# Moving the next expert's token gather one chunk earlier, and its one-hot transposes behind it, in a mixture-of-experts decoder kernel

## The reference

```
def moe_ffn(h, router_w, wg, wu, wd):
    B, S, D = h.shape
    t = h.reshape(B * S, D)
    logits = (t @ router_w).astype(jnp.float32)
    top_vals, top_idx = lax.top_k(logits, TOP_K)
    gates = jax.nn.softmax(top_vals, axis=-1)
    combine = jnp.sum(jax.nn.one_hot(top_idx, N_EXPERTS, dtype=jnp.float32) * gates[..., None], axis=1)
    y = jnp.zeros((B * S, D), jnp.float32)
    for e in range(N_EXPERTS):
        y = y + combine[:, e:e + 1] * swiglu(t, wg[e], wu[e], wd[e]).astype(jnp.float32)
    return y.astype(h.dtype).reshape(B, S, D)
```

## Time and profile before

| | |
|---|---|
| median of 3 runs | 1327.45 us (1326.04 to 1327.48) |
| span of the profiled execution | 1324.5 us |
| profiled execution's own time beside its span | not listed apart; the median of the runs is 2.95 us above the span |
| PE busy with matmuls | 1248.4 us, 94% |
| DVE busy | 1011.2 us, 76% |
| ACT busy | 793.3 us, 60% |
| first gate matmul of expert 0 | at 493.29 us |

### The profile page before, as it was taken

The page is one execution under the profiler, slowest core; times in us unless marked ns, Lnnn a source line. Parts: engine busy times, 40 slices in busy tenths (PEclk is TensorE's granted clock), DMA queues, the critical chain, the costliest instruction groups (busy, mean ns, idle before and its releaser), DMA issues.

```text
span 1324.5 us, 16360 instructions
## 1 busy us (share of the span) xinstructions
PE 1248.4 (94%) x6062; PEld 1037.6 (78%) x6062; DVE 1011.2 (76%) x988; ACT 793.3 (60%) x710; POOL 0.2 (0%) x4
## 2 busy tenths in 40 slices
PE   6998999999999869999999999989999998999996
PEld 4787788889787758887887887877887886887885
DVE  6878664444685778789788788887889886888885
ACT  4455354434446347677677677666667665667663
POOL 0000000000000000000000000000000000000000
PEclk9999899999999889999999999999999998999998
DMA  9842245546563138899899899898989998989970
GB/s 359 306 159 96 95 161 188 159 128 199 169 225 115 59 100 308 274 354 376 278 335 399 280 343 386 286 336 309 313 299 379 330 306 313 333 285 380 349 259 35
DMA packets 158798, 343.19 MB, mean 259 GB/s; under 512 B 5824, under 2 KB 47040, under 8 KB 158720
## 3 DMA queue, kind: packets, MB, share of 16 engines
q1 hardware_dynamic: 158720, 342.10, 74.3%
HBM read 341.02 MB, written 1.05 MB: 258 GB/s over the span
## 4 chain that ended last, share of the span: by engine, by line
PE 83%; DVE 10%; ACT 4%; issue 2%; DMA 0%; SPq 0%; DVEq 0%; ACTq 0%
PE ps L415 26%; PE ps L417 25%; PE ps L416 25%; DVE wlo L290 5%; ACT whi L283 3%; PE ps L644 1%; PE ps L465 1%; DVE scaled L1114 1%; PE ps L766 1%; PE ps L767 1%; PE ps L440 1%; PE ps L741 1%; PE ps L740 1%; DVE stlo L1124 1%; PE ps L514 0%
## 5 line engine op out<-in xcount | busy, mean ns | idle before, releaser
L290 DVE TENSOR_TENSOR wlo<-raw,whi 128x2048 fp32r<-128x2048 f32 (+3 forms) x356 | 741.3, 2100 | 237.6 <-ACT whi L283 237.2
L283 ACT ACTIVATE whi<-raw 128x2048 fp32r<-128x2048 f32 (+3 forms) x356 | 625.5, 1765 | 342.8 <-PE ps L417 341.3
L415 PE MATMUL ps<-whi,sthi 128*128 128x512 f32 (+4 forms) x1232 | 468.9, 381 | 21.7 <-DVE wlo L290 14.4
L417 PE MATMUL ps<-whi,stlo 128*128 128x512 f32 (+4 forms) x1232 | 457.9, 372 | 3.6 <-issue 3.6
L416 PE MATMUL ps<-wlo,sthi 128*128 128x512 f32 (+4 forms) x1232 | 458.5, 372 | 0.0
L415 PEld LDWEIGHTS ps<-whi,sthi 128*128 128x128 f32 x1232 | 233.8, 190 | 72.7 <-issue 22.7
L417 PEld LDWEIGHTS ps<-whi,stlo 128*128 128x128 f32 x1232 | 233.6, 190 | 39.0
L416 PEld LDWEIGHTS ps<-wlo,sthi 128*128 128x128 f32 x1232 | 234.3, 190 | 34.3
L415 PE MATMUL ps<-whi,hidhi 128*128 128x512 f32 (+1 forms) x440 | 176.6, 401 | 14.2 <-DVE wlo L290 11.4
L416 PE MATMUL ps<-wlo,hidhi 128*128 128x512 f32 (+1 forms) x440 | 172.3, 391 | 0.0
L417 PE MATMUL ps<-whi,hidlo 128*128 128x512 f32 (+1 forms) x440 | 172.2, 391 | 0.0
(11 more groups left out here) (191 smaller groups left out, 608.0 us busy)
## 6 DMA issues: line engine op xcount, KB each, us to landing
raw<-in_expert_w_down SPq DMA_DIRECT2D x80, 1024.0 KB, 6.8
raw<-in_expert_w_gate SPq DMA_DIRECT2D x64, 1024.0 KB, 7.3
raw<-in_expert_w_up SPq DMA_DIRECT2D x64, 1024.0 KB, 8.0
raw<-in_w_in SPq DMA_DIRECT2D x18, 1024.0 KB, 9.6
raw<-in_expert_w_gate SPq DMA_DIRECT2D x16, 768.0 KB, 6.1
raw<-in_expert_w_up SPq DMA_DIRECT2D x16, 768.0 KB, 5.1
raw<-in_dense_w_down SPq DMA_DIRECT2D x10, 1024.0 KB, 4.9
raw<-in_expert_w_gate SPq DMA_DIRECT2D x16, 640.0 KB, 4.2
```

Of the source, the lines that this page charges most:

```text
L283: eng.activation(whi[0:rows, n % SPLIT, 0:k * cols], raw[0:rows, n % RAW, 0:k * cols], ACT.Copy).then_inc(sem("hi_ready"), 1)
L290: eng.tensor_tensor(wlo[0:rows, n % SPLIT, 0:k * cols], raw[0:rows, n % RAW, 0:k * cols], whi[0:rows, n % SPLIT, 0:k * cols].bitcast(F32), ...
L415: pe.matmul(dst, xh, wh, start=start, stop=False)
L417: return pe.matmul(dst, xl, wh, start=False, stop=stop)
```

## The change

The four steps of the gather move one chunk earlier. `collect` goes from chunks 2 and 3 to 1 and 2, and `gather` with its scaling and splitting goes from chunks 4 and 5 to 3 and 4. `onehot_in` goes from chunk 1 to chunk 0. The transposes of the one-hot matrix go from chunk 2 to chunk 5, and ACT's copy of them too. The waits follow: bank 3 is now free for `collect` when the one-hot matrix of the expert before has been copied, and free for `turn_onehot` when both gathered halves have been scaled. For expert 0, whose gather stands ahead of the loop, `turn_onehot` so waits for the second scaled half instead of the first. The change is cut here to its core:

```
             def turn_onehot(k, it):
-                pe.wait_ge(sem("onehot_ready"), counted(k + 1, it, 2))
-                if k:
-                    pe.wait_ge(sem("gathered_scaled"), counted(2 * k, it, 4))
+                pe.wait_ge(sem("gathered_scaled"), counted(2 * k + 2, it, 4))
             def collect(k, it, half, bank=3):
-                if k == 0 and isinstance(it, int):
+                if half == 0:
+                    pe.wait_ge(sem("onehot_ready"), counted(k + 1, it, 2))
+                    if k:
+                        pe.wait_ge(sem("onehot_T"), counted(k, it, 2))
+                elif k == 0 and isinstance(it, int):
                     pe.wait_ge(sem("onehot_ready"), 1)
-                elif half == 0:
-                    pe.wait_ge(sem("onehot_T"), counted(k + 1, it, 2))
...
-                        if c == 2:
-                            if before:
-                                scatter(k - 1, it, 1 - par, 1)
+                        if c == 2 and before:
+                            scatter(k - 1, it, 1 - par, 1)
+                        if c == 5:
                             turn_onehot(k + 1, it)
...
-                        if c in (2, 3):
-                            collect(k + 1, it, c - 2)
-                        if c == 4:
+                        if c in (1, 2):
+                            collect(k + 1, it, c - 1)
+                        if c == 3:
                             gather(k + 1, it, 0)
...
-                        if c == 4:
+                        if c == 3:
                             gather(k + 1, it, 1)
...
-            pe.wait_ge(sem("gathered_scaled"), 1)
             turn_onehot(0, 0)
...
-                    if c == 2 and what == ("up", 0):
+                    if c == 5 and what == ("up", 1):
                         onehot_out(k + 1, it, 1 - par)
-                    if what == ("down", 1) and c in (2, 3):
-                        rows_copy(k + 1, it, c - 2)
-                    if (c, what) in ((4, ("down", 1)), (5, ("up", 0))):
-                        gathered_hi(k + 1, it, 1 - par, c - 4)
+                    if what == ("down", 1) and c in (1, 2):
+                        rows_copy(k + 1, it, c - 1)
+                    if (c, what) in ((3, ("down", 1)), (4, ("up", 0))):
+                        gathered_hi(k + 1, it, 1 - par, c - 3)
...
             def onehot_in(k, it):
                 if k:
-                    dve.wait_ge(sem("collected"), counted(2 * k, it, 4))
+                    dve.wait_ge(sem("onehot_turned"), counted(k, it, 2))
...
-                    if what == ("gate", 1) and c == 1:
+                    if what == ("gate", 1) and c == 0:
                         onehot_in(k + 1, it)
-                    if (c, what) in ((4, ("down", 0)), (5, ("gate", 1))):
-                        gathered_scale(k + 1, it, c - 4)
-                    if (c, what) in ((4, ("down", 1)), (5, ("up", 1))):
-                        gathered_rest(k + 1, it, 1 - par, c - 4)
+                    if (c, what) in ((3, ("down", 0)), (4, ("gate", 1))):
+                        gathered_scale(k + 1, it, c - 3)
+                    if (c, what) in ((3, ("down", 1)), (4, ("up", 1))):
+                        gathered_rest(k + 1, it, 1 - par, c - 3)
```

## The result

The changed kernel took 1328.42 us in the median of 14 runs (1326.07 to 1331.89), the kernel before 1325.38 us (1322.32 to 1329.21) in as many. The ratio is 1.0025, 95% interval 1.0015 to 1.0034, so the change costs about 3.3 us, with 2.0 and 4.5 as bounds. That is slower by 0.25%. The forecast was +2.6 us, and 1328.42 lies in its range, 0.1 us above the lower end; it misses the forecast's own 1329.0 to 1331.0. The forecast was counted from the 1327.45 us of three runs, and the same kernel's median in 14 runs is 2.1 us lower, so the difference of the two kernels is the better measure.

A forecast was written before the change was run, and what follows sets the result against it. PE's gapless stream (busy 94%) was taken as the bound, so work added there shows in full. Experts +1.8 us and start +0.8 made +2.6, so 1327.45 became 1330.1 us, range 1328.3 to 1332.6.

The forecast's parts named there:

- the forecast's own 1329.0 to 1331.0: Whole kernel: bounds of the summed forecast, from experts at 1.1 to 2.3 us, start 0.7 to 0.9, small items 0.3.
- The experts' term: All eight experts: gather transposes in chunk 3 cost 0.43 us each, one-hot move gains 0.22 (0.12 in one): +1.8 us.
- The freed chunk 5 gains nothing: Before down 0 of chunk 5: taking away DVE's scaling and remainder, 0.68 us each, gains nothing, as ACT ends last.
- The four transposes in chunk 3 cost 0.43 us and chunk 4 gives nothing back: Gather half 0 moved: +0.43 us an expert in chunk 3; chunk 4's wait at down 0 only grows, 0.19 to 0.6.
- The one-hot term: One-hot transposes from chunk 2 into chunk 5's wait: -0.22 us in seven experts, -0.12 in expert 0.
- The start's +0.8: Ahead of expert 0: transposes wait for the second scaling, so the first gate product starts 0.7 to 0.9 us later.
- The clock: Rival, chance 0.30: clock falls behind PE's 2.4 us idle stretch ahead of expert 0, costing 1.4 to 2.8 us more.
- The new wait in chunk 4: Rival, chance 0.07: scaling or high part delays down 0, down 1 or gate 0 by 0.3 us; 2.4 more, 1332.5.
- The signs of being wrong: Chunk 5's wait falling over 0.3 us, PE waiting in chunk 3, or a new wait in chunks 0 to 3.
- The 2.95 us between span and median: Whole kernel: median of runs taken as 2.95 us above the profiled span of 1324.5 us, giving the 1327.45 start.

The follow-up runs named there:

- one number changed: Kernel before, but ahead of expert 0 the one-hot transposes wait for the second scaled half instead of the first: 1327.70 us, ratio 1.0011.
- the start as it was: Changed kernel, but ahead of expert 0 the one-hot transposes wait for the first scaled half only, as before the change: 1327.79 us, ratio 1.001.

## Why the prediction was right, and where it was not

- **The side and the size** held: +2.6 us forecast, +3.3 measured (2.0 to 4.5). The size is in part luck. The experts' term was about 0.9 us too large, and the clock's 1.6 us stood outside the sum, as a rival. With the clock's fall the prediction's own sum would have been +4.0 to +5.4.
- **The freed chunk 5 gains nothing**: shown. DVE's idle time before the split grew to 1.18 us, and with the gather alone moved the wait stayed at 1.26 us. The last to come there is ACT's chain: with its split moved ahead of the silu, down 0 came 0.22 us earlier.
- **The four transposes in chunk 3 cost 0.43 us and chunk 4 gives nothing back**: shown, 0.44 in the timeline and 0.4 an expert with the gather alone. Chunk 4's wait of 0.63 us was forecast as 0.6.
- **The one-hot term was mis-sized.** I took 0.22 us in chunk 2, and with only them moved an expert took 0.3 less. The 0.22 itself is confirmed: behind the scatter, the second product of up 0 came after 729.38 - 728.93 = 0.45 us with them and after 0.23 without. From there to the first matmul of `collect` it took 5.37 against 5.32 us. In expert 0, for which I took 0.12, it was 0.23. Where the rest lies is open. So the experts' term is 0.4 - 0.3 = 0.1 us each, and the profiles show 0.06 to 0.19, about 0.9 us in all (8 times their mean of 0.12) where I had 1.8.
- **The start's +0.8**: shown, 0.78 in the changed kernel and 0.83 with one number changed.
- **The clock** was a rival at 0.30, at 1.4 to 2.8 us, and happened in both profiles that could show it, at 1.6 and 2.5 us. My price was right and my chance too low. What I had against it, that one idle stretch alone of this length was followed by a fall, was an argument from few rows, not from a row that speaks against. The 0.50 over 894 to 897 us was a second one, behind 3.63 us of idle time. The fall isn't certain either, as the scatter at 1317.16 shows, and how often it comes is not known. The Trainium skill's advice on idle gaps ("TensorE: Matmul & The Clock Gate", section "Why this matters for your kernels"), by which the clock would hold, doesn't agree with 2.42 and 2.77 us here.
- **The new wait in chunk 4**: not there; the 1.04 us of idle time took the scaling and 0.45 us were left.
- **The signs of being wrong**: new waits did come, at gate 1 of chunk 0. They are the limit of before, 7.35 and 7.37 us behind down 0, so they don't speak against the mechanism.
- **The 2.95 us between span and median** mixed two executions. In every execution for which both are known the time is 1.7 to 2.1 us above the span. It entered only as a way to the 1327.45 and did no harm.

In the profiles the terms are 0.9 + 0.8 + 1.6 = 3.3 us. The two spans differ by 1.7 us only, since this execution came to the experts 1.23 us earlier and its two turns took 0.3 us less. The timed runs agree with the sum of 3.3, but they don't resolve its parts, and the turns of the loop move by a similar amount from profile to profile. The changed kernel and the one with the start as it was differ in nothing but one number in one wait of TensorE, ahead of the loop, and their two turns took 215.7 and 218.9 us.

The clock has a share in that, which the prediction didn't weigh. Stretches of 15 us around turns (columns as in the earlier trace rows), the kernel before and then both turns of the changed one:

```profile
890.00:905.00 15.00, 10.74 (x38) 8.45 (x39) 6.88 (x5) 5.57 (x6) 0.00 (x0) 0.77 0.75 283
```

```profile
890.00:905.00 15.00, 10.51 (x32) 7.57 (x31) 6.62 (x3) 5.16 (x4) 0.00 (x0) 0.66 0.87 340
1100.00:1115.00 15.00, 10.13 (x40) 7.63 (x40) 7.70 (x7) 7.07 (x7) 0.00 (x0) 0.89 0.80 314
```

At 0.77, 0.66 and 0.89 of the full clock these turns took 108.3, 108.9 and 106.9 us, with 5.4, 4.5 and 4.9 us of idle time in them. So the longest of the three was the one with the least idle time and the lowest clock.

## What to carry to other kernels

Before moving a piece of work off a short stage, ask what ends last in the wait there: work that lies inside a wait is free where it is, and costs its full price in the gapless stage that it is moved to. Then use the wait the other way round and move work from the gapless stages into it, but follow what is queued behind each instruction that now waits, above all where a loop or a pair ends. Weigh an idle stretch on TensorE like the 2.4 and 2.8 us here as more than its length, since the clock may fall behind it. And where a kernel has a loop, compare its turns before explaining a difference of a few us.

## What the runs showed of the hardware that was not expected

Eight more matmuls in TensorE's program, placed in an idle stretch, made each turn of a loop some 400 us later cost 2.0 and 3.1 us more. In another place they made them 3.2 and 3.6 us dearer. The loop's own instructions were the same, and the time stood in the profile as "issue", 7.88 and 4.79 us in the stretches shown. So a kernel with such a loop can change by 0.3% through code that costs nothing by itself, and a difference of that size needs the turns looked at before it is explained.

The low clock behind an idle stretch in the same place held for different lengths: products that take 5.65 us at the full clock took 7.23 and 8.10 us. The same goes for the turns, where the mean clock over 15 us was 0.66, 0.77 or 0.89 from turn to turn and kernel to kernel.
